# Seven RMS norms of a four-layer streaming encoder: mean of squares by a constant matrix on every partition, root and reciprocal there, in place of five columns spread by transpositions

## The reference, cut to what matters

```python
def rmsnorm(x, g):
    xf = x.astype(jnp.float32)
    y = xf * lax.rsqrt(jnp.mean(xf * xf, axis=-1, keepdims=True) + EPS)
    return (y * g.astype(jnp.float32)).astype(x.dtype)

    for i in range(DEPTH):
        hp = rmsnorm(xp, mix_norms[i])          # xp: 512 prompt rows, xs: 32 sample rows, 1024 wide
        hs = rmsnorm(xs, mix_norms[i])
        ...
        xp = xp + yp
        xs = xs + ys
        xp = xp + swiglu_ffn(rmsnorm(xp, ffn_norms[i]), *ffn_params[i])
        xs = xs + swiglu_ffn(rmsnorm(xs, ffn_norms[i]), *ffn_params[i])
```

## Time and profile before

| | us |
|---|---|
| median of 3 runs | 2552.59 |
| lowest and highest | 2551.68, 2553.77 |
| the profiled execution | 2551.67 |
| its span | 2549.9 |

### The profile page before, as it was taken

The page is one execution under the profiler, slowest core; times in us unless marked ns, Lnnn a source line. Parts: engine busy times, 40 slices in busy tenths (PEclk is TensorE's granted clock), DMA queues, the critical chain, the costliest instruction groups (busy, mean ns, idle before and its releaser), DMA issues.

```text
span 2549.9 us, 48137 instructions
## 1 busy us (share of the span) xinstructions
PE 2530.3 (99%) x19981; PEld 2465.5 (97%) x19981; DVE 1725.5 (68%) x2533; ACT 1197.3 (47%) x1806; POOL 171.9 (7%) x182
## 2 busy tenths in 40 slices
PE   8999999999999999999999999999999999999998
PEld 8999999999988899999998899999999999999998
DVE  5555894985555589489557556958955565884973
ACT  5453552543555455245346544524534543642543
POOL 2101000001000010000122210000011101000001
PEclk9999999999999999999999999999999999999999
DMA  4222333332433233323322232332323223333332
GB/s 119 71 69 83 108 90 101 100 92 75 122 101 100 81 92 99 108 84 98 88 71 73 73 91 83 100 108 83 95 81 89 71 69 91 104 89 91 107 89 79
DMA packets 441746, 230.68 MB, mean 90 GB/s; under 512 B 16996, under 2 KB 438080, under 8 KB 441552
## 3 DMA queue, kind: packets, MB, share of 16 engines
q1 hardware_dynamic: 439904, 226.90, 31.0%
q10 hardware_dynamic: 1200, 0.59, 0.1%
q0 software_dynamic: 448, 0.45, 0.1%
HBM read 219.03 MB, written 8.87 MB: 89 GB/s over the span
## 4 chain that ended last, share of the span: by engine, by line
PE 96%; DVE 2%; issue 1%; ACT 0%; DMA 0%; DVEq 0%; ACTq 0%
PE slot L2300 53%; PE aux L2779 11%; PE slot L2779 10%; PE aux L2783 5%; PE slot L2783 5%; PE aux L2268 2%; PE aux L2300 2%; PE aux L2681 1%; PE aux L2445 1%; PE aux L2687 1%; PE aux L2593 1%; PE aux L2531 1%; PE aux L2460 1%; DVE w_lo L1417 0%; PE aux L2463 0%
## 5 line engine op out<-in xcount | busy, mean ns | idle before, releaser
L2300 PE MATMUL slot<-xg_hi,w_hi 128*128 128x272 f32 x1792 | 387.7, 298 | 4.0 <-DVE gla_sq L1435 2.3
L737 ACT ACTIVATE w_hi<-raw 128x1024 fp32r<-128x1024 f32 (+4 forms) x217 | 250.6, 1155 | 288.8 <-PE slot L2300 270.2
L2300 PE MATMUL slot<-xg_hi,w_lo 128*128 128x272 f32 x1792 | 370.5, 288 | 0.0
L2300 PE MATMUL slot<-xg_lo,w_hi 128*128 128x272 f32 x1792 | 370.4, 288 | 0.0
L1417 DVE TENSOR_TENSOR w_lo<-raw,w_hi 128x1024 fp32r<-128x1024 f32 (+4 forms) x215 | 292.6, 1361 | 68.9 <-ACT w_hi L737 68.3
L2300 PEld LDWEIGHTS slot<-xg_hi,w_hi 128*128 128x128 f32 x1792 | 280.7, 189 | 15.7 <-issue 9.3
L2300 PE MATMUL slot<-h_hi,w_hi 128*128 128x272 f32 x1386 | 286.3, 288 | 0.6 <-issue 0.6
L2300 PE MATMUL slot<-h_hi,w_lo 128*128 128x272 f32 x1386 | 286.1, 288 | 0.0
L2300 PE MATMUL slot<-h_lo,w_hi 128*128 128x272 f32 x1386 | 285.8, 288 | 0.0
L2300 PEld LDWEIGHTS slot<-xg_lo,w_hi 128*128 128x128 f32 x1792 | 281.6, 189 | 0.0
L2300 PEld LDWEIGHTS slot<-xg_hi,w_lo 128*128 128x128 f32 x1792 | 280.6, 189 | 0.0
(11 more groups left out here) (392 smaller groups left out, 5733.3 us busy)
## 6 DMA issues: line engine op xcount, KB each, us to landing
raw<-in_l_ffn_w_out_dram SPq DMA_DIRECT2D x64, 704.0 KB, 4.6
raw<-in_l_ffn_w_in_dram SPq DMA_DIRECT2D x60, 512.0 KB, 4.9
raw<-in_l_gla_w_in_dram SPq DMA_DIRECT2D x48, 512.0 KB, 3.9
ffn_raw_b<-in_l_ffn_w_in_dram SPq DMA_DIRECT2D x80, 256.0 KB, 3.4
ffn_raw_b<-in_l_ffn_w_in_dram SPq DMA_DIRECT2D x40, 512.0 KB, 5.3
raw<-in_l_ffn_w_in_dram SPq DMA_DIRECT2D x72, 256.0 KB, 3.2
raw<-in_l_att_w_qkv_dram SPq DMA_DIRECT2D x24, 512.0 KB, 3.8
raw<-in_l_lru_w_in_dram SPq DMA_DIRECT2D x24, 512.0 KB, 3.8
```

The costliest lines, as they stand in the source:

```text
L737: act.activation(w_hi[par][:, 0:kt, :], raw[par][:, 0:kt, :], ACT.Copy).then_inc(s_hi, 1)
L2300: ins = pe.matmul((slot[par] if bank is None else bank)[:, hf, 0:HALF], w[par][:, k, :], a[:, k0 + k, hf * HALF:(hf + 1) * HALF], start=(k ...
```

## The change

For the seven norms of `first_two`, the five columns and the five transpositions go. `stat_mean` multiplies `sq_sum` by `mean_h` at the place where `stat_sum` stood (512 columns into A3, 32 into A2), ACT takes the root of both pieces straight into `rstd` with a scale of 256/1024, and DVE takes the reciprocal of `rstd` in place. The hook in the second block goes.

```diff
             def stat(k):
                 act.wait_ge(s_st1, k)
-                act.activation(rms5[:, :], A2[:, 480:481 + QT], ACT.Sqrt, bias=eps[:, 0:1]).then_inc(s_rms, 1)
+                act.activation(rstd[:, 0:SEQ], A3[:, :], ACT.Sqrt, bias=eps[:, 0:1], scale=GLA_DV / D_MODEL)
+                act.activation(rstd[:, SEQ:TOK], A2[:, 0:DEC_SEQ], ACT.Sqrt, bias=eps[:, 0:1],
+                               scale=GLA_DV / D_MODEL).then_inc(s_rms, 1)
...
-            def stat(k, dst):
-
-                stat_inv(k)
-                stat_take(k, dst)
+            def stat_root(k):
+
+                dve.wait_ge(s_rms, k + 1)
+                dve.reciprocal(rstd[:, :], rstd[:, :]).then_inc(s_rstd, 1)
+                dve.wait_ge(s_rstd, k + 1)
...
                 if b0:
                     split(b0 + 1, (b0 + 1) % 2, XT)
-                    stat_inv(stat_of[i, "mix"])
                     gate_weights()
-                    stat_take(stat_of[i, "mix"], rstd)
+                    stat_root(stat_of[i, "mix"])
                     read(b0, b0 % 2, GL["low_in"], GATE_ROWS)
...
                 split(b0 + 1, (b0 + 1) % 2, XT)
-                stat(stat_of[i, "mix"], rstd)
+                stat_root(stat_of[i, "mix"])
                 take(0)
...
                 if hf == 0 and u == 0:
-                    stat_inv(stat_of[i, "ffn"])
                     t_sum(i, 0)
                     t_sum(i, 1)
-                    stat_take(stat_of[i, "ffn"], rstd)
+                    stat_root(stat_of[i, "ffn"])
...
-            def stat_sum(k, mean):
+            def stat_mean(k):
 
                 pe.wait_ge(s_sq, k)
-                for t in range(QT + 1):
-                    cols = slice(t * P, (t + 1) * P) if t < QT else slice(TOK - P, TOK)
-                    ins = pe.matmul(A2[:, 480 + t:481 + t], sq_sum[:, cols], mean[:, 0:1], start=True, stop=True)
-                ins.then_inc(s_st1, 1)
+                pe.matmul(A3[:, :], mean_h[:, :], sq_sum[:, 0:SEQ], start=True, stop=True)
+                pe.matmul(A2[:, 0:DEC_SEQ], mean_h[:, :], sq_sum[:, SEQ:TOK], start=True, stop=True).then_inc(s_st1, 1)
...
-                hooks = {SUM_AT: lambda: stat_sum(k, mean_x)}
+                hooks = {SUM_AT: lambda: stat_mean(k)}
                 mm_block(b0, p0, XT, xg_hi, xg_lo, ready=(s_xlo, lambda n: seen + n + 1), hooks=hooks, low=low)
-                mm_block(b0 + 1, 1 - p0, XT, xg_hi, xg_lo, hooks={SPREAD_AT: lambda: stat_spread(k)})
+                mm_block(b0 + 1, 1 - p0, XT, xg_hi, xg_lo)
```

## The result

| | before | after |
|---|---|---|
| median, us | 2552.49 (6 runs, 2550.60 to 2553.77) | 2570.00 (6 runs, 2567.99 to 2571.93) |
| ratio | | 1.0068, 95% interval 1.0058 to 1.0078 |
| profiled execution, us | 2551.67 | 2571.93 |
| span, us | 2549.9 | 2570.2 |

The change makes the kernel 17.5 us slower. The forecast was 2562 with a range of 2557 to 2569, so the direction was right and the size was not: the time lies 8 us above the forecast and 1 us above the top of the range.

What follows compares the result with a forecast made beforehand. PE was taken as the bound, busy 99% of the span. FFNs +10.8, attention and LRU -1.7, GLA +0.6 sum to +9.7 on 2551.67, giving 2561.4; with medians 0.9 higher, forecast 2562, range 2557 to 2569.

Steps and rivals of the forecast that it cites:

- the unknown term: At the FFN stops: what a 3.4 us stop does to PE's clock; the sum took nothing for it.
- Rival A: PE's clock falls after the four FFN stops, 0 to 4.5 us each, middle 2.3; 2571 us; chance 0.08.
- PE's own work: At each of seven norms, PE's work falls from 1.92 to 1.08 us, saving 0.84, 5.9 over seven.
- The reciprocal: On DVE at each norm: the added reciprocal over 128 x 544 takes 3.54 us, as the head norm's does.
- An FFN norm: At each FFN's third block PE stops 3.4 us for low weights and goes on 2.7 later; four give +10.8.
- No second stop: In the FFNs, later low weights come before PE wants them, with 0.9 us to spare at the fifth block.
- Rival B: DVE does not catch up in the FFNs or GLA of layer 3; +4 to 5 us, 2567; chance 0.08.
- The attention and the LRU: At these two norms PE does not stop and each gains 0.84 us, together -1.7 us.
- The GLA of layer 3: At this norm the low weights come late; PE stops 1.4 us, net +0.6 us.
- PE busy -6: Over the whole kernel, PE's busy time falls by about 6 us.
- C: Faster: the matmul saving shows and DVE's lateness does not, at the FFN's third block; 2546.7 us; chance 0.03.
- D: Half of the FFN wait hides: each FFN norm costs 1 us or less; 2555.5 us or below; chance 0.06.

Runs made afterwards that it cites:

- the filled kernel: The changed kernel with 26 matmuls of 272 columns, result unused, put before the third block of each FFN; 2562.82 us, ratio 1.0039.
- The reordered kernels: The changed kernel with DVE's FFN sums behind the low weights (2558.56 us); then also ACT's silu earlier and the GLA's gate weights later (2554.44 us).

## Why the prediction was wrong

**The step that failed** is the one called the unknown term: what a stop of 3.4 us does to PE's clock. The prediction took nothing for it, from the nearest row, a wait of 2.31 that did no harm. Measured, the clock fell behind each of the four stops, and the slow pairs cost 1.63, 1.51, 2.69 and 1.63 us: 7.5 in all (each the distances of the slow pairs less 0.25 a pair). Of these 0.4 are the 0.1 that the first pair behind a stop takes more at full clock too, which the forecast had. The sum of 9.7, with 7.1 for the clock and 0.2 more at the GLA, gives the 17.0 that the stretches show. Rival A had the mechanism and a middle of 2.3 a stop (measured 1.5 to 2.7), but a chance of only 0.08. One row with a wait of 2.31 was read as if it set a length below which nothing happens and told something of 3.4; it did neither. That it was harmless was luck of the one execution read: behind the same wait the clock fell in five of the ten profiles. The rule that the prediction named, from the Trainium skill ("TensorE: Matmul & The Clock Gate", section "HAM oscillation — how this bites in real kernels"), should have weighed more: by it the work behind a wait that is long enough starts cold, and here the work behind the four stops ran slow, at once in three of them and 1.1 us later in the fourth.

The range was too narrow for the same reason. It was to reach over the nearer half of A, but it ended at 2569, below A's own middle of 2571, and the measured 2570.0 lies between the two.

**The steps that held:**
- *PE's own work*, 0.84 saved per norm: the two stretches in which nothing else changes give -0.85 and -0.81.
- *The reciprocal*, 3.54 like the head norm's: 3.55.
- *An FFN norm*, a stop of 3.4 and PE going on 2.7 later: 3.45, and +2.70 to +2.72 in the filled kernel, where the clock stays up. This confirms it most sharply, since it is the same kernel without the term that was missed.
- *No second stop*, DVE catches up: right, and in the filled kernel too, where the clock holds PE back no further. Rival B did not come. But the 0.9 us of room at the fifth block were small: when the stop at the third block was ordered away, they were gone, and a wait of 0.60 to 0.89 stood there.
- *The attention and the LRU*, no stop: right. At the attention DVE's first read stands 5.69 behind PE's means (642.54 to 648.23), and the prediction has it at 640.74, which is 5.69 behind its 635.05.
- *The GLA of layer 3*, a stop of 1.4 and +0.6: a stop of 1.32 by the profile, 1.49 by distance (1948.57 to 1950.31), and +0.80. The 0.1 that the first pair behind a stop takes more was left out in this sum.
- *PE busy -6*: wrong in sign, +6.2. The slow pairs, 7.5 in the four FFNs and some more in the opening of this execution, are counted as busy time. The count of busy microseconds alone would have hidden the saving.

**Rivals C and D.** C (faster) fell at its own condition: the reciprocal is not covered in the FFNs. The reordered kernels show that it can be covered at the third block, but neither of them covers it in the stretch as a whole. D (1 us or less per FFN norm) fell by the filled kernel: 2.7 each with the clock up.

**What stays open**: what decides whether the clock falls behind a stop of 2 to 3.3 us; why one of SP's issues for the LRU's gate weights is long in five of the ten kernels; and the 0.2 us in the attention.

## What to carry to other kernels

Price a new wait of the bounding engine with what its clock does afterwards: a stop of 3.3 us of PE cost 5 us here and once 6, because PE went on at half clock for 3 to 6 us. If such a stop cannot be avoided, filling it with matmuls whose result is not used gave back 7 us of the 17, and shortening it by half gave back nearly twice what was taken off the stop (3.1 for 1.7). A wait in one profile that did no harm is no price: look at the same wait in several executions.

Replacing small operations on a few columns by one over the full width is cheap on PE (1.08 for 1.92) and dear on DVE (3.55 for 0.82). Where DVE waits anyway it costs nothing (attention, LRU); where DVE is nearly full, neither of the two new orders of its work gained anything over the kernel before. Decide such a change stage by stage.

## What the hardware showed that was not expected

- PE's clock fell behind idle times of 2.13 and 2.84 us and did not behind 2.53, 3.03 and one of 3.30, in kernels whose work around the stop is the same. Behind one and the same wait of 2.16 to 2.32 in the opening it fell in five of ten profiles.
- The fall need not come with the stop: in the FFN of layer 3 of the kernel after PE runs four distances at the full pace first, and the slow pairs begin 1.1 us behind its return:

```profile
2198.97 0.41 PE L2301 MATMUL slot<-xg_hi,w_hi 128*128 128x272 f32 x2
2199.22 0.59 PE L2301 MATMUL slot<-xg_lo,w_hi 128*128 128x272 f32 x2
2199.61 0.66 PE L2301 MATMUL slot<-xg_hi,w_lo 128*128 128x272 f32 x2
```

- The slow time behind a stop was 3.4 us in three of the four FFNs of the kernel after and about 6 in the other (1579.10 to 1585.04), and it ended while PE was busy throughout.
- DVE's reciprocal goes by its columns: 1.84 us for 272, 3.25 for 496, 3.55 for 544, which is 6.3 ns for each further column. The one of 544 takes five times what a product of two tiles of that width takes (0.72).
